# An encoder step on one core: the jobs of the memory stage at every second panel, and products of ones on TensorE while the first loads are awaited

## What is computed

```python
def mem_kv(mem, g_mem, w_mem_kv, k_norm_mem):      # 256 memory tokens
    kv = rmsnorm(mem, g_mem) @ w_mem_kv            # 1024 x 1024
    k = rmsnorm(kv[..., :MEM_WIDTH]...)            # 4 heads of 128
    v = kv[..., MEM_WIDTH:]
    return k, v

for i in range(DEPTH):
    z = rmsnorm(x, g_mix[i]) @ w_in[i]
    qm = rmsnorm(z[..., MIX_WIDTH - MEM_WIDTH:]...)
    om = mem_attend(qm, mem_k[i], mem_v[i])
    # layer 0: causal pooling of z's first half; layer 1: attention with forget gates
    x = x + concat([op, om]) @ w_out[i]
    x = x + swiglu(x, g_ffn[i], w_gu[i], w_down[i])
```

## Time and profile before

| what | us |
|---|---|
| median of 3 runs (1251.15 to 1251.37) | 1251.23 |
| the profiled execution | 1250.86 |
| span of its instructions | 1249.1 |
| TensorE busy | 1213.0 |
| VectorE busy | 981.6 |
| ScalarE busy | 656.0 |

### The profile page before, as it was taken

The page is one execution under the profiler, slowest core; times in us unless marked ns, Lnnn a source line. Parts: engine busy times, 40 slices in busy tenths (PEclk is TensorE's granted clock), DMA queues, the critical chain, the costliest instruction groups (busy, mean ns, idle before and its releaser), DMA issues. The chain is left out here.

```text
span 1249.1 us, 23025 instructions
## 1 busy us (share of the span) xinstructions
PE 1213.0 (97%) x8976; PEld 1166.9 (93%) x8976; DVE 981.6 (79%) x1600; ACT 656.0 (53%) x1178; POOL 79.9 (6%) x110
## 2 busy tenths in 40 slices
PE   6999999999999999999999999999999999999996
PEld 6987999999999999999979976799999999999996
DVE  4767557999999999985765476556999999999972
ACT  6656434554555555556754366533555555555542
POOL 1000000002001001102001100000001000100102
PEclk9999999999999999999999999999999999999998
DMA  7234122225325334434443210022225423532622
GB/s 223 86 118 137 35 85 85 68 64 138 107 85 124 101 94 116 118 98 142 135 122 123 88 67 2 2 85 85 68 60 131 120 88 95 126 102 82 149 71 85
DMA packets 196915, 122.13 MB, mean 98 GB/s; under 512 B 6091, under 2 KB 189035, under 8 KB 196808
## 3 DMA queue, kind: packets, MB, share of 16 engines
q1 hardware_dynamic: 185800, 101.24, 27.7%
q0 software_dynamic: 10816, 19.36, 6.8%
q10 hardware_dynamic: 192, 0.06, 0.0%
HBM read 106.67 MB, written 6.90 MB: 91 GB/s over the span
## 5 line engine op out<-in xcount | busy, mean ns | idle before, releaser
L1050 ACT ACTIVATE WH<-RAW 128x1024 fp32r<-128x1024 f32 (+2 forms) x149 | 144.1, 967 | 145.9 <-PE ACCP L1746 119.8
L1068 ACT ACTIVATE EH<-SB 128x1024 fp32r<-128x1024 f32 (+1 forms) x116 | 112.5, 970 | 167.0 <-DVE SB L1380 82.7
L1355 DVE TENSOR_TENSOR WL<-RAW,WH 128x1024 fp32r<-128x1024 f32 (+2 forms) x149 | 166.0, 1114 | 36.4 <-ACT WH L1050 35.2
L1386 DVE TENSOR_TENSOR EL<-SB,EH 128x1024 fp32r<-128x1024 f32 (+1 forms) x116 | 128.7, 1109 | 5.2 <-ACT EH L1068 3.0
L1746 PE MATMUL ACCP<-XH,WH 128*128 128x288 f32 x512 | 111.9, 300 | 3.7 <-DVE XL L1489 3.7
L1746 PE MATMUL ACCP<-XH,WL 128*128 128x288 f32 x512 | 110.1, 297 | 0.0
L1746 PE MATMUL ACCP<-XL,WH 128*128 128x288 f32 x512 | 110.0, 297 | 0.0
L1756 PE MATMUL MISC<-BH,EH 128*128 128x288 f32 x360 | 106.8, 297 | 1.6 <-DVE EL L1386 1.5
L1756 PE MATMUL ACCP<-BH,EH 128*128 128x288 f32 x360 | 106.6, 296 | 0.0
L1756 PE MATMUL ACCP<-BL,EH 128*128 128x288 f32 x360 | 106.2, 295 | 0.0
L1756 PE MATMUL MISC<-BL,EH 128*128 128x288 f32 x360 | 106.2, 295 | 0.0
(11 more groups left out here) (318 smaller groups left out, 3437.9 us busy)
## 6 DMA issues: line engine op xcount, KB each, us to landing
RAW<-in_w_gu SPq DMA_DIRECT2D x88, 512.0 KB, 4.0
RAW<-in_w_down SPq DMA_DIRECT2D x48, 384.0 KB, 4.1
RAW<-in_w_in SPq DMA_DIRECT2D x16, 512.0 KB, 4.4
RAW<-in_w_mem_kv SPq DMA_DIRECT2D x16, 512.0 KB, 3.7
RAW<-in_w_out SPq DMA_DIRECT2D x16, 512.0 KB, 4.0
X<-PC POOLq DMA_DIRECT2D x48, 144.0 KB, 2.8
RAW<-in_w_down SPq DMA_DIRECT2D x16, 256.0 KB, 2.9
RAW<-in_w_kv SPq DMA_DIRECT2D x8, 512.0 KB, 3.8
```

Of the source, the lines that this page charges most:

```text
L1050: a.activation(panel_in(WH, w % SPLIT_SLOTS, p), panel_in(RAW, p % RAW_SLOTS, p), ACT.Copy).then_inc(split_ready(w, True)[0], 1)
L1068: a.activation(EH[:, first:first + n, 0:nh], mixtures(s)[:, first:first + n, 0:nh], ACT.Copy).then_inc(block_hi, n)
L1355: v.tensor_tensor(panel_in(WL, w % SPLIT_SLOTS, p), panel_in(RAW, p % RAW_SLOTS, p), panel_in(WH, w % SPLIT_SLOTS, p), ALU.subtract).then_ ...
L1386: v.tensor_tensor(EL[:, first:first + n, 0:nh], mixtures(s)[:, first:first + n, 0:nh], EH[:, first:first + n, 0:nh], ALU.subtract).then_in ...
```

## The change

Three things change. First, in the memory stage of both layers `step_group` is called for every second panel only; the other panels are made alone, and `now` advances half as often. Second, in layer 0 the turns "cmk" and "state" move from behind the stage to behind its fifth and sixth panel (e = 1, j = 0 and 1). Third, TensorE multiplies the matrix ONES with itself into a part of ACCP that nobody reads: 24 times before it waits for the constants, 36 times after the first part of X, and 36 times after the vectors. Before the 24 it waits for ONES alone, which VectorE sets first.

```diff
-                step_group(now, make)
-                now += 1
+                if j % 2:
+                    step_group(now, make)
+                    now += 1
+                else:
+                    make()
                 spread(1)
+                if layer == 0 and (e, j) == (1, 0):
+                    assert not fill
+                    turn("cmk", layer=layer)
+                elif layer == 0 and (e, j) == (1, 1):
+                    turn("state")
+                    store("state", m=count["job"])
                 if (e, j) == (0, HK - 1):
                     add("key_squares", layer=layer, g=g)
...
         if layer == 0:
-            assert not fill
-            turn("state")
-            store("state", m=count["job"])
-            turn("cmk", layer=layer)
             while pend:
...
+            def turn_over(n):
+
+                for _ in range(n):
+                    t.matmul(ACCP[:, 1, 1, 0:P], ONES[:], ONES[:], start=True, stop=True)
+
+            pe.wait_ge(consts_dve, 1)
+            turn_over(24)
             pe.wait_ge(consts, 6)
             pe.wait_ge(consts_dve, DVE_CONSTS)
...
                         turn_blocks(s.m, [(ps[:, 0, 0:NVEC], VROW[:], NVEC)])
+                        turn_over(36)
...
+                        if s.t == 0:
+                            turn_over(36)
```

## The result

Six runs of the changed kernel took 1253.02 to 1256.89 us, with a median of 1254.88; six of the kernel before, on the same chip, took 1251.15 to 1252.25, with a median of 1251.59. The ratio is 1.0028, with a 95% interval of 1.0018 to 1.0037: the change makes the kernel slower by about 3.3 us. The forecast was 1246.2, and the range of 1245.0 to 1248.0 didn't hold the time.

What follows compares the result with a forecast made beforehand. TensorE, busy 97% of the span, was taken as the bound. Gains of 2.16 + 2.9 + 0 = 5.0 us bring the profiled 1250.86 to 1245.8; the median, 0.37 above, was forecast at 1246.2, range 1245.0 to 1248.0.

Steps and rivals of the forecast that it cites:

- the price of the ones: At the start: one 128 x 128 product of ones takes 0.08 us at the fast clock, 0.13 at the slow.
- part 3 of X turned later than 11.64: Sign at the start that the prediction is wrong: the transposes of X's part 3 run later than 11.64.
- The term, taken as 0: Products of ones at the start: from a loss of 1.7 to a gain of 0.1 us, taken as 0.
- the ones hold up X: Rival at the start: ones at 0.24 us each delay X's parts some 8 us, giving 1254; chance 0.04.
- the clock falls behind the scores: Rival, layer 0: the new idle stretch brings a slow stretch of 2.8 us, costing at most 1.4: 1247.6; chance 0.07.
- Layer 0's stage: Memory stage of layer 0: scores issued at 104.6, not 108.83; VectorE lets 2.16 us of gain through.
- the idle stretch: Behind layer 0's first scores: TensorE stands idle for some 2.3 us while VectorE works.
- Layer 1's: Memory stage of layer 1: fewer waits between panels bring a gain of 2.9 us.
- The splits: Rival in both memory stages: splits on ScalarE or VectorE come late and lose 2 us: 1248.2; chance 0.11.
- The wait for ACC: Second group at the start: TensorE arrives 0.8 us earlier at the sum over ACC and waits for it.
- The two terms together: Gains of the memory stages, 2.16 us in layer 0 and 2.9 in layer 1, summed as 5.0.
- nothing moves: Rival: slack in layer 0's attention and the kv groups takes the gain back, giving 1251; chance 0.03.

Runs made afterwards that it cites:

- the run that fills the gap: Full change without its ones, plus 16 products of ones behind the four first scores of layer 0: 1245.58 us, ratio 0.9962.
- the last 36 alone: Kernel before with only the 36 products of ones behind the vectors: 1250.9 us, ratio 0.9994.
- the turns left in place: Jobs at every second panel, no ones, turns of U and CMK behind the eighth panel as in the kernel before: 1245.91 us, ratio 0.9956.
- stage alone: Full change without any product of ones: 1248.82 us, ratio 0.998.
- layer 1 alone: Kernel before with jobs at every second panel in layer 1 only, no ones: 1249.01 us, ratio 0.9979.
- the run with half the ones: Kernel before with 12, 18 and 18 products of ones at the three places: 1252.78 us, ratio 1.0006.
- the run with transposes in the middle: Kernel before with the three groups of ones, the middle 36 replaced by transposes of part 0 of X: 1255.04 us, ratio 1.0024.
- the run on prices: Kernel before with 36 products of ones behind the vectors, then 24 each of five other shapes: 1267.52 us, one run.

## Why the prediction was wrong

**The step that failed first** is the price of the ones: "with TensorE at work 3.5 us sooner it should rise sooner, so I take 0.08". It held two errors. The price itself was read off the columns that stream, half of a transpose, while the load of the stationary matrix sets it: 0.216 and 0.113 us at the two clocks, for 0.13 and 0.08. And the clock did not rise sooner but later: from 1.12 to 15.61, TensorE kept to 0.20 to 0.22 us an instruction throughout. With the true price and the fast clock from the beginning, which no run had, the 24 would have ended at 3.8, the 36 (from 6.2, once part 0 was turned) at 10.3, and after parts 1 and 2 part 3 would have come at 12.4, 0.8 late; this is worked out, not run. By the same working, the other 6 us came with the slow clock. The prediction's own sign of being wrong, part 3 of X turned later than 11.64, came: even part 1 is turned only at 15.61. The term, taken as 0 with a loss of 1.7 as its bound, measured 7.05 in the profile and 6.1 by medians. The bounds of the price, 0.06 to 0.24, did hold it, but the bound of the term was taken at 0.13; the rival at the upper end, "the ones hold up X", "decides from about 0.19 us a product on", named the mechanism and the threshold, and had 0.04. That its own time of 1254 came near is luck in part: it put the start at a loss of 8 us, where 6.1 to 7.05 was measured, and it didn't have the 3 us of the clock behind the scores.

**The second step** is a rival, "the clock falls behind the scores", with the mechanism right and the size wrong: "costs at most 1.4". That bound was half of the 2.8 us window at the start. Here the clock stayed down for 6.8 us and cost 3.1 (22.55 for 19.46), shown by the run that fills the gap. What spoke against it, that TensorE's share is not full in that part, doesn't hold: in the window of the kernel before, 116 to 120, TensorE is busy for 4.00 of 4.00 us.

**What was right.** Layer 0's stage: no waits for PD or SQL; the stretch from the first panel to the scores 26.16 us for a forecast of 26.1 (78.49 to 104.6); STAT 28.72 us after the first panel (85.54 to 114.26) for 28.86; the idle stretch 2.14 for 2.3. Layer 1's: 2.96 in the full change and 2.98 by itself, for 2.9. The splits did not become the bound. The wait for ACC that was to swallow a faster first group came (0.5 us in the full change, 0.45 with the last 36 alone). The two terms together are 5.0 on paper. The stage as forecast, with the gap filled, gained 5.8 by medians (1251.37 less 1245.58), and with the turns left in place 5.5 (1251.37 less 1245.91). That "nothing moves" in the stages behind is excluded too. One reading of the rows was too short: the list of waits that the prediction went by also holds 3.4 us for PR (five waits), 2.0 for HBL and 1.5 for EL in the later stages, each more than the 1.3 and 1.1 that it calls the largest after SQL. No term hung on it.

**By parts**: +6.1 for the ones, −5.5 for the jobs at every second panel, and +2.9 for the early turns of U and CMK (stage alone 1248.82 less 1245.91), together 3.5, where 3.3 were measured. Two of the three parts of the change lose. The early turns lose through the clock alone: with the gap filled, their version takes 1245.58, and without them it is 1245.91.

**What stays open.** Why the clock stayed low through the ones at the start is not settled. With no ones ahead of X it was up by part 3, turned at about 11.6, in five of seven profiles, and in the two others (layer 1 alone, the last 36 alone) only at about 13. Behind 30 ones it rose at about 13, behind 60 at about 18 (two profiles), and with transposes of X for the middle 36 at about 9 (one profile). Transposes and products of ones differ in their data and in the kind of instruction, and the two were not tried apart. Nor do ones count for nothing: 16 of them in the gap behind the scores, and 36 ahead of the first group, kept the clock at 1.00 (the latter in the full change and in the run with them alone).

How long the slow stretch behind the scores lasts differs from run to run, as the mean clocks of the stage alone suggest; only one run of each version was profiled. The scatter by itself says less: 4.2 us over 11 runs of the stage alone, 3.9 over 6 of the full change and 1.7 over 5 with the turns in place, but also 3.2 over 15 runs of the kernel before.

## What to carry to other kernels

Idle products given to TensorE have their own price: weigh each by the load of its stationary matrix, at the slow clock, and give it no more than fits in the wait that it stands in, since the excess lands on the path. Before moving small work out of a wait, look at what else the wait has behind it: if another engine sets the end, the move gains nothing, and here it turned two short gaps into one longer one, behind which the clock fell. And when several small changes come as one, price each by itself; here the halved calls of the jobs were the gain, and the rest gave it back.

## What the runs showed of the hardware

- A product of 128 x 128 in this type behind its own weight load: 0.113 us at the full clock, 0.216 at half; 0.1 with 32 columns moving; 0.067 with a stationary matrix of 32 columns; 0.217 with 512 columns moving.
- An idle stretch of 2.13 us on TensorE, with the scores before it and the next ones behind it, was followed by 6.8 us at a granted clock of 0.50, beginning 1.5 to 1.6 us after the work had begun again; 1.27 and 0.26 us in the same place were not.
- In the run with half the ones, a gap of 1.68 us ahead of the first group, with 18 products of ones before it, was followed by a granted clock of 0.50 from about 19.5 on.
- With no ones ahead of X the clock rose at different times in different profiles: part 3 of X was turned in 1.06 to 1.07 us in five of them, and in one (layer 1 alone) still in 1.90.
- The clock fell with TensorE busy without a gap, twice under products of ones: at 19 in the run with transposes in the middle, and at 21 in the run on prices.

```profile
21.00:22.00 1.00, 1.00 (x8) 1.00 (x7) 1.00 (x3) 1.00 (x3) 0.00 (x0) 0.60 1.17 351
...
23.00:28.00 5.00, 5.00 (x24) 5.00 (x25) 4.47 (x8) 3.01 (x6) 0.00 (x0) 0.50 0.49 148
```

- In the first stretch of a run the column of the granted clock reads 1.00 while instructions take twice their time (eight transposes 1.94 us for 1.06): there the durations tell the clock, and the column doesn't.
